# First attention: bias and mask added on VectorE in the instruction that forms the running minimum

## What is computed

```python
rel = jnp.arange(CHUNK)[:, None] + A_LEFT_CHUNKS * CHUNK - jnp.arange(A_BAND)[None, :]
bias = rel_table[:, jnp.clip(rel, -A_REL_CLIP, A_REL_CLIP) + A_REL_CLIP]
valid = jnp.repeat(band_idx >= A_LEFT_CHUNKS, CHUNK, axis=1)
s = jnp.einsum("bcqhd,bckhd->bchqk", qc, kb).astype(F32) * (dh ** -0.5) + bias.astype(F32)
s = jnp.where(valid[None, :, None, None, :], s, NEG_INF)
p = jax.nn.softmax(s, axis=-1).astype(v.dtype)
o = jnp.einsum("bchqk,bckhd->bcqhd", p, vb)
```

## Time and profile before

| | us |
|---|---|
| runs: median (lowest, highest) | 2807.58 (2803.63, 2822.59) |
| the profiled execution: span from the first to the last instruction | 2817.3 |
| TensorE busy in it | 2571.8 (91%) |
| VectorE, ScalarE, POOL busy | 1247.4, 919.5, 38.1 |
| first attention: first score to start of last value product | 170.9 to 260.2 |
| second attention: first to last maximum | 1241.1 to 1300.8 |

### The profile page before, as it was taken

How to read it: one execution, slowest core, us unless ns; L and a number is a source line. 1 busy time by engine, 2 the same in 40 slices (tenths; PEclk the granted TensorE clock), 3 DMA queues, 4 the chain that set the end, 5 groups by cost and what they waited for, 6 DMA issues and landing times.

```text
span 2817.3 us, 43050 instructions
## 1 busy us (share of the span) xinstructions
PE 2571.8 (91%) x17909; PEld 2228.2 (79%) x17909; DVE 1247.4 (44%) x1583; ACT 919.5 (33%) x1210; POOL 38.1 (1%) x110
## 2 busy tenths in 40 slices
PE   7999889999989777778689998989899999999996
PEld 5966688888878666647688897979798997996995
DVE  3344442333253667443378686868686001001001
ACT  3244222222232333243166574747474000000001
POOL 5000000000000000000000000000000000000000
PEclk9999589999999888889699999999999999997998
DMA  5300012232221000010099696969696884882660
GB/s 167 104 16 1 30 56 95 90 123 97 85 89 57 2 2 2 17 45 1 24 348 361 221 360 220 362 220 361 220 361 209 269 269 153 268 267 87 228 224 30
DMA packets 328450, 432.31 MB, mean 153 GB/s; under 512 B 7375, under 2 KB 290870, under 8 KB 328270
## 3 DMA queue, kind: packets, MB, share of 16 engines
q1 hardware_dynamic: 327150, 427.37, 45.1%
q0 software_dynamic: 1120, 2.20, 0.3%
HBM read 427.43 MB, written 2.12 MB: 152 GB/s over the span
## 4 chain that ended last, share of the span: by engine, by line
PE 86%; DVE 7%; ACT 3%; issue 3%; DMA 1%; SPq 0%; DVEq 0%; ACTq 0%
PE bank L595 83%; PE bank L598 3%; DVE arena L1628 2%; DVE slot L1628 1%; ACT w_high L1550 1%; DVE w_low L1628 1%; ACT arena L1281 0%; DVE arena L1655 0%; DMA slot<-in_moe_w_gate_dram 0%; DVE small L1677 0%; DVE xs L1628 0%; DVE xg_low L1628 0%; DMA xs<-in_x_dram 0%; ACT arena L1451 0%; ACT arena L1328 0%
## 5 line engine op out<-in xcount | busy, mean ns | idle before, releaser
L595 PE MATMUL bank<-arena 128*128 128x144 f32 (+9 forms) x3584 | 587.3, 324 | 29.1 <-DVE arena L2117 16.6
L595 PEld LDWEIGHTS bank<-arena 128*128 128x128 f32 (+3 forms) x3584 | 459.7, 191 | 121.6 <-issue 75.3
L1628 DVE TENSOR_TENSOR w_low<-slot,w_high 128x2048 fp32r<-128x2048 f32 x172 | 394.2, 2292 | 321.7 <-ACT w_high L1262 274.4
L595 PE MATMUL bank<-w_high,xg_high 128*128 128x256 f32 x1120 | 324.7, 290 | 17.2 <-issue 9.1
L595 PE MATMUL bank<-w_low,xg_high 128*128 128x256 f32 x1120 | 319.4, 285 | 0.0
L595 PE MATMUL bank<-w_high,xg_low 128*128 128x256 f32 x1120 | 319.0, 285 | 0.0
L595 PE MATMUL bank<-arena,slot 128*128 128x144 f32 (+3 forms) x2304 | 298.2, 312 | 14.8 <-ACT slot L1472 14.8
L595 PEld LDWEIGHTS bank<-arena,slot 128*128 128x128 f32 (+2 forms) x2304 | 284.7, 193 | 28.0 <-ACT slot L1472 16.0
L1628 DVE TENSOR_TENSOR arena<-arena,bank 128x256 f32<-128x256 f32 (+3 forms) x134 | 64.0, 477 | 527.2 <-PE bank L595 527.2
L1628 DVE TENSOR_TENSOR w_low<-arena,w_high 128x2048 fp32r<-128x2048 f32 x105 | 240.7, 2292 | 64.3 <-ACT w_high L1550 64.3
L595 PE MATMUL bank<-h_high,w_high 128*128 128x512 f32 x592 | 236.9, 400 | 7.7 <-DVE h_low L1628 7.7
(11 more groups left out here) (317 smaller groups left out, 3404.8 us busy)
## 6 DMA issues: line engine op xcount, KB each, us to landing
slot<-in_moe_w_gate_dram SPq DMA_DIRECT2D x64, 1024.0 KB, 6.2
arena<-in_moe_w_down_dram SPq DMA_DIRECT2D x64, 1024.0 KB, 6.1
slot<-in_moe_w_up_dram SPq DMA_DIRECT2D x56, 1024.0 KB, 6.8
arena<-in_moe_w_up_dram SPq DMA_DIRECT2D x56, 1024.0 KB, 6.7
arena<-in_moe_w_gate_dram SPq DMA_DIRECT2D x48, 1024.0 KB, 6.0
slot<-in_moe_w_down_dram SPq DMA_DIRECT2D x48, 1024.0 KB, 6.6
slot<-in_e_w_in_dram SPq DMA_DIRECT2D x12, 1024.0 KB, 5.3
slot<-in_ff_w_gate_dram SPq DMA_DIRECT2D x11, 1024.0 KB, 5.2
```

What stands on the lines that cost most here:

```text
L595: return pe.matmul(o, lhsT, rhs, start=start, stop=True, skip_group_check=True)
L1628: return dve.tensor_tensor(o, a, b, op)
```

## The change

The bias tile is built differently. POOL negates and reverses the row of 640 (`bias_rev`), stores it to DRAM once for each of 128 partitions and each head (2.62 MB instead of 20 KB), and loads it back with a row step of 639, so that `bias_w` has the negated bias with queries on partitions and keys along the row. It then waits for these loads and writes a large positive number into the last 64 columns of the first 64 rows, which is the mask of the diagonal block; its other constants come after that. `flip` goes, and POOL's two instructions for it.

TensorE computes only the product of q and k, with q negated by ScalarE in the copy that scales it. VectorE's maximum becomes a tensor_tensor_reduce: it adds the score in the bank to the last n columns of the head's bias tile, writes the sum (the negated score) into `probs`, and gives the minimum of the sum, which is the negated maximum of the score. ScalarE's Exp reads `probs` instead of the bank, with scale -1. The score's bank is free after the minimum. VectorE waits for the transposes of the step that used the `probs` buffer before, which ScalarE did until now. The second attention's instructions stay.

```diff
--- before.py
+++ after.py
@@ -227,7 +227,6 @@
             slot_at.append(nc.sbuf_base - 4 * SLOT)
         xs = sb("xs", [P, NT, D])
         ident = sb("ident", [P, P])
-        flip = sb("flip", [P, P])
         chunk_mask = sb("chunk_mask", [P, P])
         causal_mask = sb("causal_mask", [P, P])
         cum_incl = sb("cum_incl", [P, P])
@@ -288,7 +287,7 @@
         conv_out = region(24600, CONV_TILES, SEQ)
         probs = region(28696, 3, SEQ)
         probsT = [region(2048 * i, NT, SEQ) for i in range(2)]
-        bias_ext = region(24600, 640, rows=HEADS)
+        bias_ext, bias_rev = region(24600, 640, rows=HEADS), region(25300, 640, rows=HEADS)
         x_tok, xdt = region(8192, NT, B_WIDTH), region(10240, NT, B_WIDTH)
         y_tok, cbT = region(12288, NT, B_WIDTH), region(16384, B_GROUPS, NT, SEQ)
         decay = [region(20480 + 2048 * i, NT, SEQ) for i in range(2)]
@@ -381,7 +380,7 @@
         banks = [ctx.enter_context(nc.psum_tensor(f"bank{i}", [P, 512], F32)) for i in range(8)]
         turn_banks, acc = banks[0:4], banks[4:8]
 
-        ext_d = nc.dram_tensor("bias_ext_d", [HEADS, 640], F32)
+        ext_d = nc.dram_tensor("bias_ext_d", [HEADS, P, 640], F32)
 
         def cols8(dram, lo, n):
             return dram[:, lo:lo + n].rearrange("(k p) n -> p k n", p=P)
@@ -517,15 +516,15 @@
             pool.dma_start(bias_ext[:, 0:384], a_rel_bias[0, :, 129:513]).then_inc(sem("rel_loaded"), 16)
             pool.wait_ge(sem("rel_loaded"), 16)
             link(pool.tensor_copy(bias_ext[:, 384:640], bias_ext[:, 383:384].to_broadcast([HEADS, 256])))
-            pool.dma_start(ext_d[:, :], bias_ext).then_inc(sem("rel_stored"), 16)
+            link(pool.tensor_scalar(bias_rev, bias_ext[:, ::-1], -1.0, None, ALU.mult))
+            pool.dma_start(ext_d[:, :, :], bias_rev.unsqueeze(1).to_broadcast([HEADS, P, 640])).then_inc(sem("rel_stored"), 16)
             pool.wait_ge(sem("rel_stored"), 16)
 
             for h in range(HEADS):
-                src = bass.AP(ext_d, 640 * h, [[1, P], [1, SEQ]])
+                src = bass.AP(ext_d, 640 * P * h + P, [[639, P], [1, SEQ]])
                 pool.dma_start(bias_w[:, h, :], src).then_inc(sem("bias_loaded"), 16)
-
-            link(pool.memset(flip[:, :], 0.0))
-            select(flip[:, :], ALU.not_equal, 1.0, -(P - 1), [[1, P]], 1)
+            pool.wait_ge(sem("bias_loaded"), 16 * HEADS)
+            pool.memset(bias_w[0:CHUNK, :, SEQ - CHUNK:], -MASKED).then_inc(sem("bias_masked"), 1)
 
             link(pool.memset(chunk_mask[:, :], 0.0))
             link(pool.memset(chunk_mask[0:CHUNK, CHUNK:P], MASKED))
@@ -669,7 +668,7 @@
 
                 for i in range(HEADS * NT + 3):
                     if i < HEADS * NT:
-                        b, former = tile("probs_ready", first + i + 1)
+                        b, former = tile("probs_ready" if first else "max_ready", first + i + 1)
                         pe.wait_ge(*former)
                         score(b, i // NT, i % NT).then_inc(sem("scores_full"), 1)
 
@@ -725,16 +724,12 @@
 
             if upto >= 2:
                 pe.wait_ge(sem("const_ready"), 1)
-                pe.wait_ge(sem("bias_loaded"), 16 * HEADS)
                 pe.wait_ge(sem("qk_stored"), 8)
                 pe.wait_ge(sem("v_stored"), 8)
 
                 def score_a(b, h, t):
                     rows = slice(64 * (h % 2), 64 * (h % 2) + 64)
-                    mm(b[:, 0:P * (t + 1)], qT[rows, h // 2, P * t:P * (t + 1)], kT[rows, h // 2, 0:P * (t + 1)], True)
-                    for k in range(t + 1):
-                        mm(b[:, P * k:P * (k + 1)], bias_w[:, h, P * (t - k):P * (t - k + 1)], flip[:, :], False)
-                    return mm(b[:, P * t:P * (t + 1)], ident[:, :], chunk_mask[:, :], False)
+                    return mm(b[:, 0:P * (t + 1)], qT[rows, h // 2, P * t:P * (t + 1)], kT[rows, h // 2, 0:P * (t + 1)], True)
 
                 attention(0, score_a, lambda h, k: v_a[:, k, HD * h:HD * (h + 1)], 0)
 
@@ -1313,11 +1308,11 @@
                     if i < HEADS * NT:
                         n = P * (i % NT + 1)
                         act.wait_ge(sem("max_ready"), first + i + 1)
-                        if first or i >= 3:
+                        if first:
 
                             act.wait_ge(sem("probsT_full"), first + i - 2)
-                        b = bank["probs_ready", first + i + 1]
-                        act.activation(probs[:, i % 3, 0:n], b[:, 0:n], ACT.Exp, bias=small[:, 48 + i % 4:49 + i % 4],
+                        b = bank["probs_ready", first + i + 1] if first else probs[:, i % 3, :]
+                        act.activation(probs[:, i % 3, 0:n], b[:, 0:n], ACT.Exp, bias=small[:, 48 + i % 4:49 + i % 4], scale=1.0 if first else -1.0,
                                        accum_out=small[:, 52 + i % 4:53 + i % 4]).then_inc(sem("probs_ready"), 1)
                     u = i - 2
                     if u >= 0:
@@ -1335,7 +1330,7 @@
             for c in range(8):
                 act.wait_ge(sem("qk_full"), c + 1)
                 act.activation((qT if c < 4 else kT)[:, c % 4, :], bank["qk_stored", c + 1][:, :], ACT.Copy,
-                               scale=HD ** -0.5 if c < 4 else 1.0).then_inc(sem("qk_stored"), 1)
+                               scale=-HD ** -0.5 if c < 4 else 1.0).then_inc(sem("qk_stored"), 1)
                 if c % 2:
                     next_high(E_IN, c // 2)
             act.wait_ge(sem("w_dt_loaded"), 16 * KT)
@@ -1674,8 +1669,14 @@
                     if i < HEADS * NT:
                         n = P * (i % NT + 1)
                         dve.wait_ge(sem("scores_full"), first + i + 1)
-                        dve.tensor_reduce(small[:, 48 + i % 4:49 + i % 4], bank["probs_ready", first + i + 1][:, 0:n], AX, ALU.max,
-                                          negate=True).then_inc(sem("max_ready"), 1)
+                        low = small[:, 48 + i % 4:49 + i % 4]
+                        if first:
+                            dve.tensor_reduce(low, bank["probs_ready", first + i + 1][:, 0:n], AX, ALU.max, negate=True).then_inc(sem("max_ready"), 1)
+                        else:
+                            if i >= 3:
+                                dve.wait_ge(sem("probsT_full"), i - 2)
+                            dve.tensor_tensor_reduce(out=probs[:, i % 3, 0:n], in0=bank["max_ready", i + 1][:, 0:n], in1=bias_w[:, i // NT, SEQ - n:],
+                                                     op0=ALU.add, op1=ALU.min, scale=1.0, scalar=-MASKED, accum_out=low).then_inc(sem("max_ready"), 1)
                     u = i - 1
                     if 0 <= u < HEADS * NT:
                         n = P * (u % NT + 1)
@@ -1740,6 +1741,7 @@
 
             step(dve.scalar_tensor_tensor(out=dt_keep, in0=dt_row[0], scalar=0.0, in1=dt_row[1], op0=ALU.max, op1=ALU.add))
             if upto >= 2:
+                dve.wait_ge(sem("bias_masked"), 1)
                 attention(0, 0)
                 step(dve.memset(ones_row, 1.0))
                 dve.wait_ge(sem("pv_done"), HEADS)
```

## The result

| | us |
|---|---|
| kernel before, 20 runs: median (lowest, highest) | 2813.47 (2803.63, 2828.73) |
| changed kernel, 20 runs | 2830.01 (2811.48, 2842.20) |
| ratio | 1.0046, 95% interval 1.0029 to 1.0062 |
| profiled execution: before, after | 2817.3, 2818.3 |

The prediction said 2791, at most 2807. A second comparison of the same two kernels (e11_after_again) gave 1.0018 (0.9994 to 1.0042), so how much slower the change is stays less sure than the first interval says; faster by the forecast 0.6% it is in neither. The attention itself did about what was forecast; the store to DRAM, which the prediction put at nothing, cost more than the attention gained.

A forecast was written before the change was run, and what follows sets the result against it. TensorE was taken to bound the first attention, 10.63 us a head, falling to 8.29: six heads at 2.34 plus 1.3 and 1.1 for the end heads save 16.4 us, from median 2807.6 to 2791; range 2773 to 2807.

The forecast's parts named there:

- Work at nothing: List of changes forecast to cost or gain no time, among them the larger store, hidden behind the input projection.
- Each tile is asked for a whole split before its own turn: Input projection: SP's weight loads share DMA engines with the store in 17 to 56 us, but their lead was to protect them.
- POOL's constants with 16 us to spare: POOL behind the store: constants end at 72 to 86 us, hidden behind the input projection, 16 us spare in the worse case.
- Rival 4: POOL or the store is late, needing 16 us beyond the worse case; every further us costs one; chance 0.03.
- 28 records gone: TensorE, each first-attention head: 10 bias and 4 mask products removed, 3.11 us; period without any wait 7.01 us.
- The minimum: VectorE's tensor_tensor_reduce in the first attention: 0.75 us at 512 plus 0.10 for handing out the minimum.
- the first wait: TensorE's wait ahead of the third tile's transposes in each first-attention head, forecast at 0.85 us.
- Rival 1: VectorE's minimum runs at the scan's rate, 1.21 us at 512; heads take 8.9 to 9.1 us, 11 to 13 saved; chance 0.14.
- First and last head: Ends of the first attention: 1.3 us (0 to 2) saved in the first head, 1.1 in the last.
- Rival 2: TensorE's clock falls in the first attention; a half-clock head costs 5.7 us more, all cold gives 2830; chance 0.07.
- The later stages should take what they took, except for their clock: Expected sign: stages after the first attention keep their durations apart from clock changes, with no cost forecast.
- Rival 3: More than forecast: heads of 7.9 us save 20 us, a warmer stage behind 5 to 10 more, 2779 or less; chance 0.12.

The follow-up runs named there:

- e11_after_again: The changed kernel itself, unaltered, run again beside the version that stores from 128 partitions; 2829.28 us, ratio 1.0018 to the kernel before.
- e5_sixteen_rows: Changed kernel with each bias row on two partitions, so 16 partitions are stored 64 times each, same 2.62 MB; ratio 0.9951 to the kernel before.
- e6_half_volume: Changed kernel with the 8 rows stored 64 times each (1.31 MB), both halves of each bias tile loaded from the same copies; ratio 0.9962 to the kernel before.
- e4_128_rows: Changed kernel with the bias rows first spread to 128 partitions, each stored 8 times, same 2.62 MB; ratio 0.9940 to the kernel before.
- e9_warm_pause: The 128-partition version of the changed kernel plus 24 unread identity products in TensorE's pause before the first attention's first transposes; 2801.96 us, 0.9931 of the kernel before.
- e1_attention_alone: Changed kernel with the store back at 20 KB and the old load row step, so bias values are wrong; 2863.96 us, 1.0137, total not comparable.
- e3_two_halves: Changed kernel with the store issued as two DMAs of 64 copies each from the same 8 partitions; ratio 1.0019 to the kernel before.

## Why the prediction was wrong

**The step that failed** is the line on DMA and POOL under "Work at nothing". It held three statements.
- "At that pace the store takes 14 us, on half of the DMA engines 28." It took 55.9. The pace came from loads whose SBUF side is 128 partitions; the store reads 8 neighbours, and they gave 6.3 GB/s each. From 128 partitions the same volume took 10.1 us, near the 14. The bound from the nearest row was a bound on engines, and the resource was another one.
- "Each tile is asked for a whole split before its own turn", so the weights were to be safe. The tile that took 52.6 us landed at 75.1, so it was asked for at about 22.5, and ScalarE stood for it from 54.6: a lead of 32 us. This was the costly sentence: nothing in it asked how the two queues share an engine, where the tile first got no turn for some 15 us on the shared ones and then one packet for each of the store's. A store of 28 us would indeed have hidden, as the prediction said (e5_sixteen_rows and e6_half_volume: tiles up to 28.5 us, no wait); one of 55 did not.
- POOL's constants with 16 us to spare: they ended at 115.0 instead of 72 to 86, and still nobody waited for them. Rival 4 had the right object, the store, but looked for its price on POOL's queue, and gave it 0.03. The price was on SP's.

18.4 us late at the first score is 14.2 us of waiting and about 3 of clock. Behind the wait the changed kernel has

```profile
79.30:86.00 6.70, 6.63 (x16) 5.21 (x17) 2.31 (x2) 0.57 (x1) 0.00 (x0) 0.53 1.05 370
```

which is 0.47 x 6.7 / 0.5 = 6.3 us at half clock, and half of that, 3.1 us, is lost; before the wait (60 to 65 us) and from 86 us on the clock is 1.00. About 1 us is left unexplained.

**The attention was right.** 16.4 us were forecast, 15.4 measured as the mean of three, 17.8 in e4_128_rows (89.3 - 71.5), where the last value product starts at 242.4 us against the forecast 244. That the sum comes so near is in part luck: a head saves 10.63 - 7.81 = 2.82 us and not 2.34, 2.9 us more in six, and stretches at half clock and the ends took back 3.9 in the mean of the three profiles and 1.5 in e4_128_rows. Term by term:
- 28 records gone: 7.81 - 0.54 - 0.21 = 7.06 us without waits, forecast 7.01.
- The minimum: 0.69 + 0.08 us, forecast 0.75 + 0.10, and the lower bound was 0.69. It took the first wait to 0.54 instead of 0.85 and the second to 0.21 instead of 0.43. VectorE is busy 3.84 us a head, not about 5.
- Rival 1, the scan's rate of 1.21 us, is out. One source in PSUM and one in SBUF did not halve the rate, so the Trainium skill's rule on two SBUF sources ("Vector Engine (DVE) Microarchitecture Reference", section "Points that are easy to get wrong") did not bear on it; what the page names is one instruction form, and the trace records the new instruction as `CUSTOM_DVE_ANT_0`, so no run here tells whether the rule is meant for it. That an accumulator comes out in a second instruction, the trace shows: `DVE_READ_ACCUMULATOR2_ANT`, 83 ns.
- First and last head: the first is cold behind a pause of 5.6 us (forecast 4.7), which e9_warm_pause prices at 4.1 us (195.50 - 191.25, less the 0.17 us that its first score is earlier). In e4_128_rows the first two heads together save 2.8 us, one warm head's worth, so the first saved nothing of the 1.3 forecast (0 to 2).

**Rival 2, the clock, came half true.** The prediction held against it that the second attention stays at 1.00 while busy 88%. The first attention, busy 7.05 of 7.80 us in the changed kernel, 90%, lost its clock in none to two heads of a profile besides the first, 3 us each and not the 5.7 forecast, since each fall is shorter than a head: e1_attention_alone, with two of them in a row, has a mean clock of 0.77 from 199 to 229 us, which is 0.23 x 30 / 0.5 = 14 us at half clock in 21.6 us of two heads. With the pauses filled no profile of three had such a head. But what the prediction held against the rival is true as well: in all 19 profiles the second attention has no head at half clock behind its first (a period is 7.81 to 7.84 us, the last 7.4), and it waits longer, 0.65 and 0.27 us. So waits in a head don't account for the falls by themselves, and the two stages were not as alike as the prediction took them to be; what in the first attention's products makes the difference (its score is a product 64 rows deep without a mask product behind it) was not tried. The changed kernel's windows of a warm head and of a stretch with a cold one:

```profile
224.40:232.20 7.80, 7.05 (x28) 3.25 (x27) 3.84 (x16) 3.91 (x12) 0.00 (x0) 1.00 0.00 0
235.00:240.00 5.00, 4.86 (x12) 2.18 (x13) 2.37 (x12) 2.64 (x10) 0.00 (x0) 0.58 0.01 2
```

**"The later stages should take what they took, except for their clock"** left the exception unpriced: +7.5 us on average in the stage behind. Rival 3 had priced only the luck of it, 5 to 10 us back.

Two slips in the prediction's numbers carry nothing: eight heads at 5.7 us more give 2837, not 2830, and "faster by over 1%" has 0.13 where the rival that it needs has 0.12.

## What to carry to other kernels

A DMA's time follows not from its volume and its engines alone but also from how many SBUF partitions give it (here 8 neighbours against 16 and 128). A broadcast store from 8 partitions wants its rows spread first (here 55.9 us to 10.1). A transfer that is itself hidden is not free: count what it does to every transfer that shares its engines, packet by packet, and hold the delay against that transfer's lead; here a tile asked for early landed only with the store's end, so the safe number was the store's whole time. And where TensorE's waits grow, look at the granted clock in several profiles, not in one; short throwaway products in the waits may keep it: in a long pause they did in four profiles of four, in the short waits of a head three profiles of three agree and don't prove it.

## What was not expected of the hardware

- Eight neighbouring SBUF partitions as a DMA source gave about 50 GB/s together (0.20 MB in 4 us), with 8 or 16 engines, and sixteen gave 0.41 MB in 4 us; the engines read as busy meanwhile, 92% at 0.20 MB. It is a limit that neighbours share: the store's last packets took 0.37 us instead of 0.78.
- Queues of an engine alternate by the packet, 308 packets of 5 KB against 306 of 1 KB, but a transfer that comes second first gets no turn: none in 8 us read in the changed kernel, none in 26 us of e3_two_halves.
- tensor_tensor_reduce with one source in PSUM runs at the plain reduction's rate: 691 ns for 512, 558 for 384, 425 for 256, then 83 ns for the accumulator.
- TensorE's clock fell in a stage that is 90% busy with waits of 0.54 and 0.21 us in a head of 7.81 (1.00 to 0.50, single heads), and stayed at 1.00 when these waits were filled, 24 heads of 24. The Trainium skill ("TensorE: Matmul & The Clock Gate", section "A second HAM failure mode: psum-queue depth-cycling") reports such an oscillation where short idles come often. These runs agree in the first attention; the second, with waits of 0.65 and 0.27 us in 7.83, held 1.00 behind its first head in 19 profiles.
- The stage behind runs at 0.50 for most of its time although TensorE's row is busy, in any kernel here. The same instructions took 83.3 us (e5_sixteen_rows) and 98.3 (e6_half_volume) behind last value products at 242.7 and 243.0 us.
